# Six sets of matmul rows moved to other distances from the weight tiles, modulo 256 bytes

## The reference, cut to what matters

```python
mem_n = rmsnorm(mem, mem_norm)
for l in range(DEPTH):
    h = h + mixer(rmsnorm(h, mix_norm[l]))               # convolution + pooling / sparse attention + recurrence
    h = h + memory_cross_attn(rmsnorm(h, xattn_norm[l]), mem_n, wq[l], wkv[l], wo[l])
    h = h + peer_ffn(rmsnorm(h, peer_norm[l]), peer_wq[l], peer_keys[l], peer_u[l], peer_v[l])
h = rmsnorm(h, final_norm)
for layer in range(DEPTH):
    h = h + mix(_rmsnorm(h, attn_norm_2[layer]))         # latent + dilated / windowed attention
    gu = _rmsnorm(h, ffn_norm_2[layer]) @ w_gate_up[layer]
    h = h + (silu(gu[..., :D_FF]) * gu[..., D_FF:]) @ w_down[layer]
```

## Time and profile before

| | us |
|---|---|
| median of 3 runs | 2812.21 (2805.3 to 2812.48) |
| the profiled execution | 2813.5 |
| its span in the trace | 2811.2 |
| TensorE, matmuls | 2714.5 busy |
| TensorE, weight loads | 2544.1 busy |
| VectorE | 2053.1 busy |
| ScalarE | 1454.5 busy |
| GpSimd | 177.8 busy |

### The profile page before, as it was taken

The page is one execution under the profiler, slowest core; times in us unless marked ns, Lnnn a source line. Parts: engine busy times, 40 slices in busy tenths (PEclk is TensorE's granted clock), DMA queues, the critical chain, the costliest instruction groups (busy, mean ns, idle before and its releaser), DMA issues.

```text
span 2811.2 us, 57248 instructions
## 1 busy us (share of the span) xinstructions
PE 2714.5 (97%) x19552; PEld 2544.1 (90%) x19552; DVE 2053.1 (73%) x4430; ACT 1454.5 (52%) x2378; POOL 177.8 (6%) x141
## 2 busy tenths in 40 slices
PE   7999999999999999989999999999999989999998
PEld 6999899999988888979998999988888889999998
DVE  8557997886566667876699888567776877666665
ACT  5455345444555555555544444455555565446544
POOL 0004000000000000000374000000000100000000
PEclk9999999999999999999999999999999999999999
DMA  5445566455766665424456555676666525563454
GB/s 190 176 157 184 204 215 213 174 182 195 261 242 242 242 242 179 149 78 165 165 182 217 191 172 183 218 258 242 242 242 242 187 81 182 190 230 117 177 184 178
DMA packets 140451, 546.19 MB, mean 194 GB/s; under 512 B 15784, under 2 KB 81592, under 8 KB 83616
## 3 DMA queue, kind: packets, MB, share of 16 engines
q1 hardware_dynamic: 63216, 455.38, 44.8%
q10 hardware_dynamic: 73728, 67.14, 7.4%
q0 software_dynamic: 3376, 21.88, 2.0%
HBM read 505.53 MB, written 40.91 MB: 194 GB/s over the span
## 4 chain that ended last, share of the span: by engine, by line
PE 78%; DVE 15%; DMA 2%; ACT 2%; issue 2%; DVEq 0%; ACTq 0%; SPq 0%
PE bank L796 23%; PE bank L797 23%; PE bank L798 23%; PE bank L1016 4%; DVE wL L551 4%; DMA ring<-in_w_stream 2%; PE bank L917 1%; ACT wH L540 1%; PE bank L937 1%; DVE pr_eq L1969 1%; DVE pr_eq L1971 1%; DVE pr_m L1973 1%; PE bank L928 1%; DVE pr_m L1924 0%; DVE pr_i L1924 0%
## 5 line engine op out<-in xcount | busy, mean ns | idle before, releaser
L551 DVE TENSOR_TENSOR wL<-ring,wH 128x1024 fp32r<-128x1024 f32 x809 | 988.1, 1224 | 605.5 <-ACT wH L540 602.5
L540 ACT ACTIVATE wH<-ring 128x1024 fp32r<-128x1024 f32 x864 | 907.3, 1055 | 423.2 <-DMA ring<-in_w_stream 252.6
L796 PE MATMUL bank<-hnH,wH 128*128 128x256 f32 x3528 | 1003.3, 284 | 34.5 <-DVE wL L551 26.6
L797 PE MATMUL bank<-hnL,wH 128*128 128x256 f32 x3528 | 984.0, 279 | 0.0
L798 PE MATMUL bank<-hnH,wL 128*128 128x256 f32 x3528 | 983.5, 279 | 0.0
L796 PEld LDWEIGHTS bank<-hnH,wH 128*128 128x128 f32 x3528 | 667.5, 189 | 45.7 <-issue 22.9
L797 PEld LDWEIGHTS bank<-hnL,wH 128*128 128x128 f32 x3528 | 667.2, 189 | 0.5 <-issue 0.2
L798 PEld LDWEIGHTS bank<-hnH,wL 128*128 128x128 f32 x3528 | 665.1, 189 | 0.0
L796 PE MATMUL bank<-wH,wgtH 128*128 128x512 f32 x1024 | 398.5, 389 | 0.3 <-DVE wgtL L2010 0.3
L798 PE MATMUL bank<-wH,wgtL 128*128 128x512 f32 x1024 | 398.4, 389 | 0.0
L797 PE MATMUL bank<-wL,wgtH 128*128 128x512 f32 x1024 | 398.3, 389 | 0.0
(11 more groups left out here) (411 smaller groups left out, 3535.3 us busy)
## 6 DMA issues: line engine op xcount, KB each, us to landing
ring<-in_w_stream SPq DMA_DIRECT2D x432, 1024.0 KB, 4.9
act_parked<-act_out ACTq DMA_DIRECT2D x256, 128.0 KB, 3.0
act_in<-act_parked ACTq DMA_DIRECT2D x256, 128.0 KB, 2.7
sw_bias<-in_c_swa POOLq DMA_DIRECT2D x1, 4096.0 KB, 15.7
relb_rows<-rel_table POOLq DMA_DIRECT2D x1, 2048.0 KB, 10.0
h_parked<-h POOLq DMA_DIRECT2D x2, 1024.0 KB, 6.3
h_back<-h_parked POOLq DMA_DIRECT2D x2, 1024.0 KB, 6.2
od_relb<-relb_rows POOLq DMA_DIRECT2D x2, 1024.0 KB, 7.4
```

The costliest lines, as they stand in the source:

```text
L540: eng.activation(wH[:, b % NBUF, :], raw(b), ACT.Copy).then_inc(w_high, 1)
L551: eng.tensor_tensor(wL[:, b % NBUF, :], raw(b), wH[:, b % NBUF, :].bitcast(F32), ALU.subtract).then_inc(w_low, 1)
L796: pe.matmul(dst, lh, rh, start=start, stop=False, skip_group_check=True)
L797: pe.matmul(dst, lh, rl, start=False, stop=False, skip_group_check=True)
```

## The change

Four pairs (`mem`, `att_OT`, `pr_h`, `od_y`) and `ff_a` were two tiles each, high and low. Each becomes one tile of 8 elements more, and `pair` takes the two halves out of it from an offset of 2, 4 or 6 elements (8, 16 or 24 bytes). Where it begins is also moved by `pr_h_before` (8240 to 8232), `ff_gap` (48 to 40) and, for the first mixer, `ev_gap` (40 to 32). By the declared sizes the rows then begin, below a multiple of 256 bytes:

| rows | before | after |
|---|---|---|
| `mem` | 64 | 40 |
| `att_OT` | 64 | 48 |
| `od_y` | 64 | 56 |
| `pr_h` | 64 | 72 |
| `ff_a` | 64 | 80 |
| `pool`, `ycat` | 64 | 96 |

The tiles laid behind `od_y` in its stage move 32 bytes up, `mem_raw` moves 32 bytes down. High and low half stay the same distance apart. No instruction is added, removed or reordered.

```diff
+        def pair(tile, first, chunks):
+
+            return [tile[:, first + s * chunks * 256:first + (s + 1) * chunks * 256].rearrange(
+                "p (a b) -> p a b", a=chunks) for s in range(2)]
...
-        _, memH, memL = stage(("mem_before", [MEM0], F32), ("memH", [DC, T], F32R), ("memL", [DC, T], F32R))
-        _, att_L, att_P, att_PT, att_O, _, att_OTH, att_OTL = stage(
+        _, mem_both = stage(("mem_before", [MEM0], F32), ("mem_both", [16 * 256 + 8], F32R))
+        memH, memL = pair(mem_both, 6, DC)
+        _, att_L, att_P, att_PT, att_O, _, att_OT = stage(
...
-            ("att_OTH", [8, 256], F32R), ("att_OTL", [8, 256], F32R))
+            ("att_OT", [16 * 256 + 8], F32R))
+        att_OTH, att_OTL = pair(att_OT, 4, 8)
...
-                ("ev_cnt", [4, 256], F32), ("ycat", [4, 256], F32), ("ev_gap", [40], F32), ("poolH", [4, 256], F32R),
+                ("ev_cnt", [4, 256], F32), ("ycat", [4, 256], F32), ("ev_gap", [32], F32), ("poolH", [4, 256], F32R),
...
-        _, pr_hH, pr_hL = stage(("pr_h_before", [8240], F32), ("pr_hH", [DC, T], F32R), ("pr_hL", [DC, T], F32R))
+        _, pr_h = stage(("pr_h_before", [8232], F32), ("pr_h", [16 * 256 + 8], F32R))
+        pr_hH, pr_hL = pair(pr_h, 6, DC)
...
-                ("od_gap", [32], F32), ("od_relb", [16, 256], F32), ("od_yH", [8, 256], F32R), ("od_yL", [8, 256], F32R),
+                ("od_gap", [32], F32), ("od_relb", [16, 256], F32), ("od_y", [16 * 256 + 8], F32R),
...
+        od_yH, od_yL = pair(od_y, 2, 8)
...
-            ("ff_gap", [48], F32), ("ff_aH", [FC, 256], F32R), ("ff_aL", [FC, 256], F32R))
+            ("ff_gap", [40], F32), ("ff_a", [2 * FC * 256 + 8], F32R))
+        ff_aH, ff_aL = pair(ff_a, 4, FC)
```

More of the change, by code:

```diff
@@ L390, in build_stacks @@
         od_q, od_ckv, od_ik, od_iq, od_hq, od_hf, od_hg, od_hi, od_ckvn, od_ckvT, od_iw, od_sel, _, od_relb, \
-            od_yH, od_yL, od_neg, od_rel, od_sc, hg_A, hg_f, hg_QL0, hg_QL1, hg_KL0, hg_KL1, hg_dq, hg_dk, \
+            od_y, od_neg, od_rel, od_sc, hg_A, hg_f, hg_QL0, hg_QL1, hg_KL0, hg_KL1, hg_dq, hg_dk, \
             hg_dq1, hg_dk1, hg_mask, hg_S, hg_X = stage(
@@ L418, in build_stacks @@
             ("sw_own", [2, 128], F32))
-        ff_s, ff_f, ff_g, ff_u, _, ff_aH, ff_aL = stage(
+        ff_s, ff_f, ff_g, ff_u, _, ff_a = stage(
             ("ff_s", [2, 256], F32), ("ff_f", [2, 256], F32), ("ff_g", [2, 256], F32), ("ff_u", [2, 256], F32),
-            ("ff_gap", [48], F32), ("ff_aH", [FC, 256], F32R), ("ff_aL", [FC, 256], F32R))
+            ("ff_gap", [40], F32), ("ff_a", [2 * FC * 256 + 8], F32R))
+        ff_aH, ff_aL = pair(ff_a, 4, FC)
         sb("arena", [P, 32768])
```

## The result

The changed kernel takes 2829.1 us (median of 5 runs, 2823.4 to 2830.3) against 2812.3 (2805.3 to 2813.9): the ratio is 1.0059, interval 1.0042 to 1.0075. It is **slower** by 0.6%. The profiled execution took 2823.35 us against 2813.5 before.

What follows compares the result with a forecast made beforehand. TensorE's matmuls (busy 97% of the span) were taken as the bound. 2820 touched matmuls x (115.6 - 115.9) gave -0.9 us, other terms 0: 2812.6 against the profiled execution, 2811 us against the median, range 2802 to 2824.

Steps and rivals of the forecast that it cites:

- what counts is the start-to-start step of lines 796 to 798: Matmuls of `product`: time follows distance between starts, 113.3 or 117.8 ns, drawn anew where TensorE stands still.
- I take the mean of the two known speeds, 115.6: Step assumed for the 2820 touched matmuls at the new distances, giving -0.9 us.
- rival 1: Touched matmuls: two speeds at the new distances too, drawn by stalls; 2804 to 2818 us; chance 0.52.
- rival 4: Touched matmuls: a third, slower speed, 122.3 ns, at some new distances; 2822, all families 2830 us; chance 0.21.
- the baseline of 115.9 ns: Mean step of the 2820 touched matmuls before the change, about 1650 slow and 1170 fast.
- Neighbours: Unbroken work behind touched stretches, such as feed-forward gate and up products, may change speed: centre 0, +-4.3 us.
- The 192 products with memory loaded: Matmuls with memory as loaded operand: 229.0 ns now, between 226.7 and 231.3; -0.4 to +0.4 us, taken as 0.
- Writers and moved tiles: ScalarE and VectorE writing shifted rows, and tiles behind `od_y` moved by 32 bytes: each taken as 0.
- Rival 3: Touched matmuls: new distances hold only the fast speed; 7.4 us off, 2805 us; chance 0.17.
- rival 2: Touched matmuls: no effect of the distance, only draws by chance; 2812 us; chance 0.10.

Runs made afterwards that it cites:

- null64: Changed kernel with all rows back at 64 bytes below the weights, packing and 32-byte shift behind `od_y` kept: ratio 1.0007 to the kernel before.
- shift32: Kernel before with every on-chip tile (rows, weights, ring) 32 bytes higher, all distances kept: ratio 1.0004.
- hn0: Kernel before with only the normed rows `hn` moved, from 64 to 0 bytes below the weights: ratio 1.0067.
- hn192: Kernel before with the normed rows `hn` 192 instead of 64 bytes below the weights: ratio 1.0044.
- hn320: Kernel before with `hn` 256 bytes higher, 320 below the weights modulo 512, still 64 modulo 256: ratio 0.9993.
- hn448: Kernel before with `hn` raised by 384 bytes, 192 below the weights modulo 256 and, by declared sizes, 192 modulo 512: ratio 1.0041.

## Why the prediction was wrong, by its own steps

The forecast was 2811 us within 2802 to 2824; the median is 2829.

- **Held: what counts is the start-to-start step of lines 796 to 798, there are two speeds at 64, and a stall draws between them.** The changed kernel, too, has both speeds in `hn`, where nothing moved (88 unbroken runs quick, 96 slow). One reading of the earlier trace rows was off: behind the start 0.21 us late the next comes 0.19 on, and the steps are 0.12 only from there.
- **Failed: "I take the mean of the two known speeds, 115.6", that is, rival 1 as the likeliest.** The two speeds belong to the distance. At 40, 48, 56, 72 and 80 bytes each set has one fixed mean step, from 119.1 to 120.8 ns, alike within 0.15 ns in every stretch of 78 matmuls or more in both traces of the changed kernel; the first mixer at 96 has 117.3 in both, and where other sets drew at 96 they never drew a quick speed. The prediction had 0.21 on this (rival 4), with 122.3 ns as its price; the true one is 119.4 in the mean over all sets, and 3.4 ns above 115.96 is just beyond the 3.0 ns it named as the point of decision. 2820 x 3.4 = 9.6 us, against 9.9 in the profiled pair.
- **Failed: the baseline of 115.9 ns.** It was read from one execution, which had drawn badly: the whole feed-forward slow. Over the seven traces with the touched sets at 64 (before, `null64`, `shift32`, `hn0`, `hn192`, `hn320`, `hn448`) the mean step is 115.96, 114.3, 114.6, 113.5, 114.9, 115.0 and 115.6, 114.8 on average; from that baseline even the assumed 115.6 would have given 2 us more instead of 0.9 less. The typical loss is then 2820 x 4.6 = 13 us, 0.46%, within both intervals. The sum was made against one draw and read off as if it were the median.
- **Neighbours: "centre 0, +-4.3"** held, 2.8 us in the profiled pair.
- **The 192 products with memory loaded**, taken as 0: held at 40 bytes (mean 228.9 before, 229.3 after, 0.1 us in all). Their upper bound of 231.3 was too low all the same: at 32, 36, 96, 144 and 192 bytes they step 233.2 to 233.7 ns.
- **Writers and moved tiles, 0**: held (`null64` for the tiles; VectorE and ScalarE are busy as before).
- **Rival 3** (only the fast speed) is refuted at all six distances, and rival 2 (no effect) by `null64` against the changed kernel.
- **The range** treated a third speed in all sets (2830) as the tail to leave out. A cause that is the same for all sets hits all at once; its case belonged inside as a whole.

The Trainium skill, "TensorE: Matmul & The Clock Gate", Step-by-step, has two independent read ports, so that loading weights takes no read bandwidth from a running matmul. The traces disagree in what follows for the time: one shape steps 113.3 to 121.4 ns by the distance of its two operands alone. The Trainium skill, "SBUF — State Buffer", Specifications, gives lines of 16 bytes with a price for each new one. Rows 8 bytes into a line (40, 56, 72: 120.0 to 120.8) are dearer than 48, 80 and 96, but 0 is as dear as they are, 8 no dearer than 0, and 36, which isn't aligned either, cheaper than 48 (117.9 and 119.2), so the line alone doesn't order the distances.

## What to carry to other kernels

When a stream of matmuls with weight loads is the bound, measure the start-to-start step by pair of operands, and treat the distance between their addresses as a parameter with a map of its own: here 64 and 144 bytes are good, and the distances without a quick speed cost 3 to 7% over the quick step of 113.3 ns. At 64 half of that advantage is left to the draw, and at 144 it starts some ten steps into a run. Don't take one execution as the baseline where speeds are drawn; read several traces of the unchanged part. And a step saved or lost on the bounding engine counts only between its waits: of 39 us of added steps 15 arrived in the profiled pair of `hn0`.

## What the runs showed of the hardware that I had not expected

- A 256-column fp32r matmul with a 128-column weight load has 113.3 ns at its quickest and 121.4 at its dearest, by the distance of streaming rows and loaded weights modulo 256 bytes; moving both together by 32 bytes changes nothing.
- Only 64, 144 and 192 of 21 distances have a quick speed; `hn` ran at it in 45 to 62% of its steps at 64, 78% at 144, 3% at 192 (11% with 256 bytes more). At 64 an unbroken run draws one speed and mostly keeps it; at 144 it begins dear and turns quick after some ten steps; at 96 stretches of one set ran at 117.3, 118.7 or 120.0 ns.
- Two quick distances in one product (high rows 64, low rows 192) gave no quick stretch, 117.8 ns in both that there were. That such a product is never quick isn't shown; that its steps aren't those of the two distances is (119.7 ns on one line).
- Which property of the memory or the engine makes this pattern is open; no run here tells it.
